# The last three expert blocks added in PSUM instead of through DRAM

## The reference

```python
hb = jax.nn.silu(xb @ w_gate[e]) * (xb @ w_up[e])            # rows of one expert
ys = hb @ w_down[e]
y = zeros.at[slot_tok].add(ys * slot_gate[:, None])          # two experts a token, weighted
h = layer_norm(ALPHA * h + y, ln_g[i, 1], ln_b[i, 1])
```

## Time and profile before

| what | before |
|---|---|
| median of three runs | 2272.41 us (2269.43 to 2273.7) |
| profiled execution, span | 2270.0 us |
| median less the profiled span | 2.4 us |
| PE busy | 2095.8 us (92%) |
| DVE busy | 801.5 us (35%) |
| ACT busy | 535.4 us (24%) |
| POOL busy | 254.3 us (11%) |
| DMA moved | 545.98 MB, mean 241 GB/s |

### The profile page before, as it was taken

How to read it: one execution, slowest core, us unless ns; L and a number is a source line. 1 busy time by engine, 2 the same in 40 slices (tenths; PEclk the granted TensorE clock), 3 DMA queues, 4 the chain that set the end, 5 groups by cost and what they waited for, 6 DMA issues and landing times. The chain is left out here.

```text
span 2270.0 us, 28982 instructions
## 1 busy us (share of the span) xinstructions
PE 2095.8 (92%) x11658; PEld 1218.6 (54%) x11658; DVE 801.5 (35%) x1734; ACT 535.4 (24%) x1229; POOL 254.3 (11%) x266
## 2 busy tenths in 40 slices
PE   7999999999999999969999898959996999989995
PEld 3446643444445577445555454548864555545552
DVE  2055325442555489452111011157745211111113
ACT  1123221022664145112212111130001212112112
POOL 0000000210111311101111111101200111111102
PEclk9999998999999999969999999979997999999998
DMA  9415243042003111259999999981134999999995
GB/s 357 143 48 186 79 165 122 32 154 74 1 1 115 75 52 73 76 225 405 426 423 424 423 422 418 417 316 45 68 149 177 366 423 424 422 424 423 423 423 203
DMA packets 101226, 545.98 MB, mean 241 GB/s; under 512 B 13424, under 2 KB 27545, under 8 KB 67146
## 3 DMA queue, kind: packets, MB, share of 16 engines
q1 hardware_dynamic: 82016, 506.22, 55.2%
q0 software_dynamic: 18592, 37.46, 4.7%
q10 hardware_dynamic: 474, 0.33, 0.1%
HBM read 538.86 MB, written 28.94 MB: 250 GB/s over the span
## 5 line engine op out<-in xcount | busy, mean ns | idle before, releaser
L847 PE MATMUL ps<-arena,ring 128*128 128x512 f32 (+8 forms) x1440 | 424.0, 453 | 9.7 <-DVE arena L2535 2.2
L1406 PE MATMUL ps<-ring,arena 128*64 128x256 f32 x3296 | 375.3, 384 | 5.8 <-ACT arena L1915 3.2
L847 PEld LDWEIGHTS ps<-arena,ring 128*128 128x128 f32 x1440 | 258.0, 193 | 164.8 <-issue 136.3
L1406 PEld LDWEIGHTS ps<-ring,arena 128*64 128x64 f32 x3296 | 233.6, 138 | 127.6 <-DMA ring<-in_moe_w_up_dram 4.4
L938 PE MATMUL ps<-ring,arena 128*128 128x512 f32 x528 | 234.3, 600 | 3.0 <-DVE arena L2303 1.3
L2660 DVE SCALAR_TENSOR_TENSOR arena<-arena,ps 128x256 f32<-128x256 f32 x78 | 32.8, 421 | 565.3 <-ACT arena L1925 565.3
L1419 PE MATMUL ps<-ring,arena 128*64 128x512 f32 x880 | 207.8, 616 | 24.4 <-DMA ring<-in_moe_w_down_dram 24.4
L1406 PE MATMUL ps<-arena 128*64 128x256 f32 x1696 | 192.6, 381 | 0.0
L3027 POOL DMA_INDIRECT assignment_rows<-arena x78 | 82.4, 1057 | 794.4 <-ACT arena L1931 765.2
L938 PEld LDWEIGHTS ps<-ring,arena 128*128 128x128 f32 x528 | 99.6, 192 | 124.9 <-issue 123.0
L1406 PEld LDWEIGHTS ps<-arena 128*64 128x64 f32 x1696 | 119.4, 137 | 60.5
(11 more groups left out here) (370 smaller groups left out, 2084.0 us busy)
## 6 DMA issues: line engine op xcount, KB each, us to landing
ring<-in_moe_w_down_dram SPq DMA_DIRECT2D x45, 2048.0 KB, 27.9
ring<-in_moe_w_up_dram SPq DMA_DIRECT2D x44, 2048.0 KB, 26.5
ring<-in_moe_w_gate_dram SPq DMA_DIRECT2D x43, 2048.0 KB, 24.2
arena<-in_moe_w_gate_dram SPq DMA_DIRECT2D x21, 2048.0 KB, 26.1
arena<-in_moe_w_up_dram SPq DMA_DIRECT2D x20, 2048.0 KB, 26.1
arena<-in_moe_w_down_dram SPq DMA_DIRECT2D x19, 2048.0 KB, 29.1
ring<-in_ada_w_dram SPq DMA_DIRECT2D x12, 2048.0 KB, 12.0
ring<-in_a_w_in_dram SPq DMA_DIRECT2D x12, 1536.0 KB, 13.9
```

Source lines behind the costliest of these rows:

```text
L847: ins = pe.matmul(dst, w, m, start=i == 0, stop=i == len(pairs) - 1)
L1406: ins = pe.matmul(ps[CAP * i:CAP * (i + 1), bank_, 256 * j:256 * (j + 1)], rows_t[:, k, :], w[:, k, 256 * i:256 * (i + 1)], start=k == 0, ...
```

## The change

Gates: DVE rewrites the ten (layer 1: eight) `block_hot` tiles with the gate in place of the one, PE makes a second set of products (`slot_gates`) behind the table's, DVE copies the gate of each slot to `gate_of`, and `yo_copy` scales by it. The rows in `ya_d` are then weighted already. ACT issues two transfers that fill `ya_d` with zeros, early in the first block's first mixer; POOL's first scatter waits for them.

Overflow: DVE computes the count ahead of the copy of the table. PE loads it and branches at the head of the stage, with the blocks in both branches; ACT and DVE branch ahead of the last block; SP and POOL branch without waiting for the last block.

Last blocks: blocks 36, 37 and 38 (`LATE` = 3) are not scattered. POOL and DVE make one-hot tiles of their tokens (`late_columns`, `late_hots`), and PE adds them, and the residual with the other blocks' rows in it, in PSUM (`late_start`, `late_blocks`). The rows of the other blocks are loaded into two slabs of the ring (tile 4's into `lnp`) as soon as block 35's scatter and the slabs' users are done, ahead of layer 1's next mixer weights, of which two were issued ahead of the rows' loads before. DVE adds them to the residual (`partial`) for all tiles of layer 0 and for tiles 0 and 3 of layer 1; POOL does tile 1 of layer 1 and PE tile 2 (`late_rest`). Statistics and normalisation read PSUM. Of layer 0's transposes DVE now copies the second half of every tile, and the tail's order becomes 0, 2, 3, 1. POOL no longer waits for the rows of the tile loads before it issues the norm rows of the tail.

```diff
+LATE = 3
+EARLY = NBS - LATE
...
+            if n == TURN[("sc_in", 0, (1, 0))]:
+                ring_at = (ring_at + 2) % RING
...
+        def yo_of(B):
+
+            return late_yo if B % NBS == NBS - 1 else yo[B % 2]
+
+        YIN_TURNS = [[TURN[("expert", l, (0, 0))] + 3 * NE - 9 + j for j in ((1, 2), (0, 1))[l]] for l in range(2)]
+
+        def yin(l, t):
+
+            if t == 4:
+                return lnp[:]
+            return slab(YIN_TURNS[l][t // 2])[:, 2 * D * (t % 2):2 * D * (t % 2 + 1)].rearrange("p (k d) -> p k d", k=2)
...
+        def late_bank(l, t):
+
+            own = bank("cg_0")
+            return (own, 6, 2 - own, 6, 2 - own)[t] if l == 0 else 2 * t
...
+        LATE_ORDER = ((4, 0, 1, 2, 3), (0, 2, 3, 1))
...
-                if l == 0:
-                    for turn in range(first + 3 * NE, first + 3 * NE + 2):
-                        dense(turn)
...
+                if l == 0:
+                    sp.wait_ge(alpha_done, 5)
+                for turn in YIN_TURNS[l]:
+                    sp.wait_ge(*consumed(turn))
                 for t in ((4, 0, 1, 2, 3), range(NT))[l]:
                     r = rows_of(t)
-                    sp.dma_start(yin[t][0:r], ya_d[l][2 * P * t:2 * P * t + 2 * r, :].rearrange("(p k) d -> p k d", k=2))\
-                      .then_inc(yin_in[t], 16)
+                    sp.dma_start(yin(l, t)[0:r], ya_d[l][2 * P * t:2 * P * t + 2 * r, :].rearrange("(p k) d -> p k d", k=2))\
+                      .then_inc(tile_in[t], 16)
...
+            for turn in range(e0 + 3 * NE, e1):
+                for i, lent in enumerate(YIN_TURNS[0]):
+                    if PREV[turn] == lent:
+                        for t in (2 * i, 2 * i + 1):
+                            partial_made(sp, 0, t)
...
+            def slot_gates(l):
+
+                n = 10 if l == 0 else 8
+                for i in range(n):
+                    r = rows_of(i // 2)
+                    pe.wait_ge(hot_ready, (0, 20)[l] + n + i + 1)
+                    ins = pe.matmul(ps[:, bank(f"table{l}") + 1, 0:NBLK], row_hot[0:r, i, :], block_hot[0:r, i, :], start=i == 0, stop=i == n - 1)
+                ins.then_inc(gates_made, 1)
...
+            def late_start(l, t):
+
+                r = rows_of(t)
+                pe.wait_ge(alpha_done, 5 if l == 0 else 9)
+                if l == 0 and t in (2, 3):
+                    pe.wait_ge(normed, 2 * LN[(3, 4 if t == 2 else 1)] + 2)
+                for h in range(2):
+                    pe.matmul(ps[0:r, late_bank(l, t) + h, :], ident[0:r, 0:r], X[0:r, t, 512 * h:512 * h + 512], start=True, stop=False)
+
+            def late_blocks(l, t):
+
+                r = rows_of(t)
+                pe.wait_ge(late_built, LATE * (l + 1))
+                for i in range(LATE):
+                    B = NBS * l + EARLY + i
+                    pe.wait_ge(yo_ready, B + 1)
+                    hot = late_meta[i] if t == 4 else late_hot[i][:, P * t:P * (t + 1)]
+                    for h in range(2):
+                        s = slice(CAP * h, CAP * (h + 1))
+                        ins = pe.matmul(ps[0:r, late_bank(l, t) + h, :], hot[s, :], yo_of(B)[s, :], start=False,
+                                        stop=i == LATE - 1 and (l, t) != (1, 2))
+                return ins
+
+            def late_sum(l, t):
+
+                partial_made(pe, l, t)
+                late_start(l, t)
+                late_blocks(l, t).then_inc(late_summed, 1)
+
+            def late_rest(l, t):
+
+                pe.wait_ge(tile_in[t], yin_landed(l, t))
+                for k in range(2):
+                    for h in range(2):
+                        ins = pe.matmul(ps[:, late_bank(l, t) + h, :], ident[:], yin(l, t)[:, k, 512 * h:512 * h + 512], start=False, stop=k == 1)
+                ins.then_inc(late_summed, 1)
...
+            def experts(l):
                 pe.wait_ge(route_ready, l + 1)
                 n_over = pe.value_load(over_i[0:1, NOVER:NOVER + 1], min_val=0, max_val=NOVER)
                 with pe.If(n_over > 0):
...
+                    blocks(l)
+                    over_blocks(l, n_over)
                 with pe.Else():
-                    pe.nop()
-
-            def experts(l):
+                    blocks(l)
+
+            def blocks(l):
+                slot_gates(l)
...
+            late_sum(0, 4)
+            late_sum(0, 0)
+            late_sum(0, 1)
             turn_tile(4, 4)
+            late_sum(0, 2)
             turn_tile(4, 0)
             turn_tile(4, 1)
+            late_sum(0, 3)
+            pe.wait_ge(normed, 2 * LN[(3, 2)] + 2)
             start_early(first, 4, 0, 0, META + P)
             turn_tile(4, 2)
             start_early(first, 4, 1, META + P, HALVES[1][0])
...
-            pe.wait_ge(alpha_done, 9)
-            for t in (1, 2):
-                for h in range(2):
-                    pe.matmul(ps[:, 2 * (t - 1) + h, :], ident[:], X[:, t, 512 * h:512 * h + 512], start=True, stop=False)
-            pe.wait_ge(gate_diags, 4)
-            for t in (1, 2):
-                pe.wait_ge(yin_in[t], 32)
-                for h in range(2):
-                    for k in range(2):
-                        ins = pe.matmul(ps[:, 2 * (t - 1) + h, :], gate_diag[:, t - 1, k, :], yin[t][:, k, 512 * h:512 * h + 512],
-                                        start=False, stop=k == 1)
-                ins.then_inc(summed_tile, 1)
+            late_start(1, 2)
+            late_sum(1, 0)
+            late_blocks(1, 2)
+            late_rest(1, 2)
+            late_sum(1, 3)
+            late_sum(1, 1)
...
+            for l in range(2):
+                z = a["zero_row"]
+                act.dma_start(ya_d[l], bass.AP(z.tensor, z.offset, [[0, 2 * (TM, S)[l]], [1, D]])).then_inc(zeros_in, 16)
...
+                n = B % NBS
+                if n < NBS - 1 and sent_before(B):
+                    act.wait_ge(yo_sent[B % 2], sent_before(B))
+                if n == 0:
+                    taken(act, f"table{B // NBS}")
+                act.activation(yo_of(B), ps[:, 6 + B % 2, :], ACT.Copy, scale=gate_of[:, n:n + 1]).then_inc(yo_ready, 1)
...
+                def last_blocks():
+                    gate_tanh(NBS * (l + 1) - 1)
+                    yo_copy(NBS * (l + 1) - 2)
+                    mark(act.activation(spec[:, 62:63], eps_col, ACT.Sqrt))
+                    yo_copy(NBS * (l + 1) - 1)
...
             bank_root(0)
             rescaled(0)
-            bank_root(1)
-            rescaled(1)
-            sums(2)
+            sums(1)
+            bank_root(2)
             rescaled(2)
             bank_root(3)
             rescaled(3)
+            rescaled(1)
...
+                step(vec.tensor_tensor(ovt, spread(cnt[0:1, 2, :], 1, NOVER), spread(expert_of[0:1, 0:NOVER], 2, NE), ALU.is_le))
+                mark(vec.tensor_copy(ovf[0:1, NOVER:NOVER + 1], cnt[0:1, 2, NE - 1:NE]))
+                step(vec.tensor_reduce(ovf[0:1, 0:NOVER], ovt, AX.X, ALU.add))
+                step(vec.tensor_scalar(ovf[0:1, 0:NOVER], ovf[0:1, 0:NOVER], float(NE - 1), None, ALU.min))
+                vec.tensor_copy(over_i[0:1, :], ovf[0:1, :]).then_inc(route_ready, 1)
...
+                for i in range(2 * nt):
+                    vec.tensor_scalar(block_hot[:, i, :], block_no, place[:, 10 + i:11 + i], gates[:, i % 2, i // 2:i // 2 + 1],
+                                      ALU.is_equal, ALU.mult).then_inc(hot_ready, 1)
...
+                done(vec, name)
+                vec.wait_ge(gates_made, l + 1)
+                ins = vec.tensor_copy(gate_of, ps[:, bank(name) + 1, 0:NBLK])
+                free(ins, name)
                 taken(vec, name)
...
+            def late_hots(l):
+
+                for i in range(LATE):
+                    vec.wait_ge(numbers_set, 9 + (2 * LATE if l else 0) + (1 + (l == 0)) * (i + 1))
+                    if l == 0:
+                        mark(vec.tensor_scalar(late_meta[i], late_meta[i], late_tok[:, i:i + 1], None, ALU.is_equal))
+                        settle()
+                    vec.tensor_scalar(late_hot[i], late_hot[i], late_tok[:, i:i + 1], None, ALU.is_equal).then_inc(late_built, 1)
...
+                step(vec.tensor_tensor(x, x, y[:, 0, :], ALU.add))
+                vec.tensor_tensor(x, x, y[:, 1, :], ALU.add).then_inc(partial_ready, 1)
...
+            partial(0, 4)
+            partial(0, 0)
+            partial(0, 1)
+            late_statistics(4)
+            late_statistics(0)
+            scaled(4)
+            partial(0, 2)
+            scaled(0)
+            late_statistics(1)
+            turn_copy(4, 4)
+            scaled(1)
+            partial(0, 3)
+            late_statistics(2)
+            turn_copy(4, 0)
+            scaled(2)
+            turn_copy(4, 1)
+            late_statistics(3)
+            scaled(3)
+            turn_copy(4, 2)
             weights_sum(0)
-            order = (4, 0, 1, 2, 3)
-            for i, t in enumerate(order):
```

(70 more changed lines are left out.)

215 lines of the change are left out of this document (100 added, 115 removed).

## The result

The changed kernel takes 2286.26 us (median of 4 runs, 2283.37 to 2288.45) against 2273.05 for the kernel before beside it: ratio 1.0058, interval 1.0042 to 1.0075, slower by 13 us. A second set of runs gave 1.0055 (1.0033 to 1.0076). The forecast was 2279 with a range of 2265 to 2292.

What follows compares the result with a forecast made beforehand. Both expert stages were taken as bound by their weight stream, leaving heads, boundary and tail to matter. Terms 0.4 + 3.4 + 1.0 + 0.0 + 0.5 + 1.2 = 6.5; 2270.0 + 6.5 + 2.4 = 2279 us, range 2265 to 2292.

Steps and rivals of the forecast that it cites:

- the heads: Start of both expert stages: count, branch and gate products delay the first transposes; +3.4 us layer 0, +1.0 layer 1.
- the forecast's own range: Whole kernel: 2274 to 2285 us, from the bounds of the forecast's heads and norm rows.
- B: Boundary and tail: an fp32 product of 512 columns costs 0.45 us, so faster, 2266.5; chance 0.10.
- C: Boundary and tail: half-height products run one after the other, 22.7 us more, 2302; chance 0.07.
- Part comes back, since PE no longer arrives cold: Head of layer 0: quicker wide products and transposes return 1.3 and 0.5 of the 5.2 us delay.
- All of it goes on the stream: Head of layer 0: the whole +3.4 us lengthens the weight stream, which never makes up a late first block.
- Rival A: Stage heads cost nothing: the stream has slack or gate products run much faster; 2274.6 us, chance 0.24.
- Boundary: Layer 0 to layer 1: PE's late products replace the wait for scattered rows; sum 0.0 us.
- D: Boundary at its floor, −6.3 us, with heads at their low bounds; 2270 us, chance 0.14.
- Tail: End of kernel: ACT's sums of tile 1 stand ahead of tile 2's root, DVE waits; +0.5 us.
- Norm rows: End of layer 1's stage: the 1 MB load goes out with two weight slabs still to come; +1.2 us.
- Zero fill: First mixer: ACT's issue of two transfers ahead of the first exponential; +0.4 us, between nothing and 3.

Runs made afterwards that it cites:

- heads2: Changed kernel with PE's count load and branch moved between blocks 29 and 30, and DVE's overflow count back behind the token lists; ratio to before 1.0021.
- branch_mid: Changed kernel with PE's overflow-count load and branch moved from the stage's head to between blocks 29 and 30; ratio to the kernel before 1.0016.
- lnp_late: Changed kernel with POOL's load of the tail's norm rows waiting for the product of block 37; ratio to the kernel before 1.0044.
- best: Changed kernel with mid-stage PE branch, count behind token lists, reordered tail, later norm-row load, two late blocks; 2265.15 us against 2272.39 before, ratio 0.9977.

## Why the prediction was right, and where its sum was off

The direction and the places were right; the sum was 7 us too small, and one term, the heads, carries 5.7 of that by the profiles. The measured 2286.26 lies a little above the forecast's own range (2274 to 2285). That it lies inside the stated one, 2265 to 2292, is partly luck: that range was drawn wide for rivals B and C, which did not come.

- **Heads, +3.4 and +1.0 forecast, +5.5 and +4.6 measured.** The late transposes were forecast as 5.2 and 3.4. The step that failed is "Part comes back, since PE no longer arrives cold": the transposes took 1.94 and the wide products 8.71 and 9.73, as before. The granted clock is still 0.57 in the window from 1020 to 1028, though the gate products end only 0.4 us ahead of the transposes. The upper bounds of 5.2 and 3.4 were thus too low as well. Layer 1's branch took longer than the row of before said (up to 4.97).
- **All of it goes on the stream.** Right in size: 2.4 MB behind to the end of the stage, 5.7 us, and that end is 5.8 us later behind T0. Rival A is refuted by the same windows and by heads2.
- **Boundary, 0.0 forecast, −1.3 measured**, order and stop included (2.1 us instead of 3.6; the clock's fall behind it, to 0.53 from 1519 to 1522, cost 1.6, forecast 1.3; in branch_mid and heads2, where it does not fall, the boundary is 47.4). Rivals B and C are refuted by one row each: 1.98 for two full products, 2.85 for six half-height ones, forecast 1.78 and 2.67; D's floor of −6.3 was not reached. A tile took 4.70 and not 4.45, 0.25 more.
- **Tail, +0.5 forecast, +0.9 measured**, and by the wait named: DVE idle 10.8 behind tile 1's sums. That its order alone was worth 6.5 us I had not said.
- **Norm rows, +1.2 forecast, 3.2 to 5.7 by the profiles.** My bounds (0 to 2.5) left out that PE's clock can fall behind a longer wait. By the rule of the Trainium skill ("DMA: Bandwidth & Descriptors", Queues, rings and completion order) the term was 1.9, nearer than my value: lnp_late's 0.45 against 1.92 of waiting agrees that queues share.
- **Zero fill, +0.4 forecast, +0.3 at ACT** (the first exponential at 109.52), nothing in the runs.
- **Left out**: the rows' loads delay the last slabs of stage 0, by 2.0 us in best and up to 3.5 with three late blocks and an early head. And the sum rested on one profile, whose T0 is chance within some 7 us.

Not settled: stage 0 ends 490.2 to 491.0 us behind T0 in branch_mid and heads2, and 491.2 to 493.6 in the five profiles with the changed kernel's head. An earlier head thus gives back only 0.2 to 3.4 us there as long as the rows' loads go out early. What those loads cost in the changed kernel itself, with its late head, no run shows: its first profile ends as late as the stream's 5.7 us alone would have it, others up to 2.4 later.

## What to carry to other kernels

Work that is put at the head of a stage bound by a stream delays the first release of a buffer, and the stream never catches up; the same branch between two blocks in the middle, where buffers stand full, cost the stream nothing (422 GB/s over it). Once a chain has been shortened, read each engine's written order again for an instruction that waits for the newest result ahead of ones whose inputs are old: a few moved lines in the tail gave back half of what the change had lost (1.0027 against 1.0055). When a wait grows, price the clock behind it too: in lnp_late's comparison the wait and the slower products after it cost about the same, though in two of the other profiles the products behind waits of 2.62 and 3.14 us kept their speed. And a load that is issued early to be ready in time can delay the one that the engine is waiting for: compare the ends with the load held back.

## What the runs showed of the hardware that I had not expected

- The same instructions end 1 to 7 us apart from profile to profile (T0 997.2 to 1004.4), mostly because the granted clock falls at different places (0.69 against 1.00 from 288 to 296 us). A piece of a profile is compared with others from a common row, not from the span's start.
- Half-height products cost 0.87 us for a block of two on a pitch of 4.70, 3.83 and 2.97 us a tile with three, two and one late blocks. What is left, 2.1, is 0.3 more than two full products of 0.89. So I estimate a fixed price of some 0.3 a tile. The Trainium skill's "TensorEngine Tiling (Array Packing)", Key Properties, has a change of tiling mode drain the array; that fits better than my reading of the earlier trace rows, though no run shows that these products change the mode, or what the 0.3 is.
- The far branch took 3.9 and 5.0 us at the head and 3.7 at the end of the stage.
